# Hybrid linear-attention layer on one core: half of one projection's depth tiles placed between the two low-rank gate products of the first head pair

## What is computed

```python
cond = silu(c); mod = cond @ w_ada + b_ada            # 6 x 1024: shifts, scales, gates
h = modulate(rms_norm(x), shift1, scale1)
proj = h @ w_in     # GLA q,k (256 each), v (512), low rank (16), gate (512); HGRN2 q,f,i,gate (512 each)
gate_logits = g_lr @ gla_gate_w2 + gla_gate_b2        # (1024,16) @ (16,256)
log_a = log_sigmoid(gate_logits) / 16                 # decay of the GLA heads
# chunkwise causal linear attention with chunks of 64, for 4 GLA and 4 HGRN2 heads
x = x + gate1 * (concat(o_gla, o_hgrn) @ w_out)
x = x + gate2 * (square(relu(modulate(rms_norm(x)) @ w_mlp1)) @ w_mlp2)
return rms_norm(x, final_norm_g)
```

## Time and profile before

| | us |
|---|---|
| median of three executions | 1175.17 |
| the profiled execution | 1174.98 |
| its span | 1173.3 |
| PE busy | 1153.5 |
| DVE busy | 808.5 |
| ACT busy | 597.3 |
| POOL busy | 441.9 |

### The profile page before, as it was taken

How to read it: one execution, slowest core, us unless ns; L and a number is a source line. 1 busy time by engine, 2 the same in 40 slices (tenths; PEclk the granted TensorE clock), 3 DMA queues, 4 the chain that set the end, 5 groups by cost and what they waited for, 6 DMA issues and landing times.

```text
span 1173.3 us, 15641 instructions
## 1 busy us (share of the span) xinstructions
PE 1153.5 (98%) x5639; PEld 956.9 (82%) x5639; DVE 808.5 (69%) x957; ACT 597.3 (51%) x898; POOL 441.9 (38%) x273
## 2 busy tenths in 40 slices
PE   7999999999999999999999999999999999999996
PEld 6878788888888888888888888888878888888885
DVE  6998766554535458367987755676796785966876
ACT  7753554646464647245655555455663433424424
POOL 1021111111111215326444442435367574765751
PEclk9999999999999999999999999999999999999999
DMA  9675241021111114341355435534624737437203
GB/s 362 235 249 162 90 145 36 19 54 36 36 36 36 37 44 137 93 159 72 117 179 167 148 117 171 179 135 140 211 72 131 245 92 265 144 130 281 78 1 144
DMA packets 148765, 152.02 MB, mean 130 GB/s; under 512 B 6228, under 2 KB 117976, under 8 KB 146008
## 3 DMA queue, kind: packets, MB, share of 16 engines
q1 hardware_dynamic: 148696, 151.12, 39.4%
HBM read 117.02 MB, written 34.08 MB: 129 GB/s over the span
## 4 chain that ended last, share of the span: by engine, by line
PE 87%; DVE 5%; issue 3%; DMA 2%; ACT 1%; SPq 1%; DVEq 0%; ACTq 0%
PE unit_bank L1321 29%; PE unit_bank L1621 8%; PE unit_bank L1622 8%; PE unit_bank L1623 8%; PE small_bank L1621 8%; PE small_bank L1622 8%; PE small_bank L1623 8%; PE small_bank L1321 3%; PE small_bank L1456 2%; DVE ada_acc L1703 2%; DMA ada_slot<-in_w_ada_dram 1%; PE small_bank L1448 1%; PE small_bank L1360 1%; DVE state L1903 1%; DMA quarter<-in_w_mlp_dram 1%
## 5 line engine op out<-in xcount | busy, mean ns | idle before, releaser
L773 POOL TENSOR_TENSOR wr_lo<-quarter,wr_hi 128x512 fp32r<-128x512 f32 x122 | 196.0, 1620 | 174.3 <-ACT wr_hi L1122 174.2
L1321 PE MATMUL unit_bank<-a_hi,w_hi 128*128 128x512 f32 x560 | 223.2, 399 | 0.0
L1321 PE MATMUL unit_bank<-a_hi,w_lo 128*128 128x512 f32 x560 | 218.4, 390 | 0.0
L1321 PE MATMUL unit_bank<-a_lo,w_hi 128*128 128x512 f32 x560 | 218.1, 389 | 0.0
L717 POOL TENSOR_TENSOR w_lo<-raw,w_hi 128x1024 fp32r<-128x1024 f32 x27 | 67.5, 2501 | 347.8 <-ACT w_hi L827 347.8
L1621 PE MATMUL unit_bank<-op_hi,wr_hi 128*128 128x512 f32 x452 | 176.5, 391 | 0.6 <-DVE op_lo L2216 0.6
L1621 PE MATMUL small_bank<-op_hi,wr_hi 128*128 128x512 f32 x452 | 176.2, 390 | 0.0
L1623 PE MATMUL unit_bank<-op_hi,wr_lo 128*128 128x512 f32 x452 | 175.9, 389 | 0.0
L1623 PE MATMUL small_bank<-op_hi,wr_lo 128*128 128x512 f32 x452 | 175.9, 389 | 0.0
L1622 PE MATMUL unit_bank<-op_lo,wr_hi 128*128 128x512 f32 x452 | 175.9, 389 | 0.0
L1622 PE MATMUL small_bank<-op_lo,wr_hi 128*128 128x512 f32 x452 | 175.8, 389 | 0.0
(11 more groups left out here) (257 smaller groups left out, 1846.1 us busy)
## 6 DMA issues: line engine op xcount, KB each, us to landing
quarter<-in_w_mlp_dram SPq DMA_DIRECT2D x128, 256.0 KB, 4.4
hidden_scratch<-hid SPq DMA_DIRECT2D x98, 256.0 KB, 2.9
ada_slot<-in_w_ada_dram SPq DMA_DIRECT2D x48, 512.0 KB, 6.5
op_full<-hidden_scratch SPq DMA_DIRECT2D x21, 1024.0 KB, 4.8
raw<-in_w_in_dram SPq DMA_DIRECT2D x29, 512.0 KB, 3.9
raw<-in_w_out_dram SPq DMA_DIRECT2D x16, 512.0 KB, 4.0
x_stage<-in_x_dram SPq DMA_DIRECT2D x8, 512.0 KB, 5.1
x_scratch<-xT SPq DMA_DIRECT2D x2, 2048.0 KB, 8.2
```

The lines of the kernel that those rows point to most:

```text
L773: pool.tensor_tensor(wr_lo[slot][:, :, :], split_source(n), wr_hi[slot][:, :, :].bitcast(F32), ALU.subtract).then_inc(wr_lo_pool, 1)
L1321: return pe.matmul(out_ap, left, right, start=start, stop=stop)
```

## The change

The first four depth tiles (12 products) of unit 2, half 0, are issued between the two `z` pieces of step 0. Step 2 issues the remaining four. The number of products and their sums are the same.

```diff
-                        half_unit(u0 + j, 1 + j, half, a_hi, a_lo)
+                        half_unit(u0 + j, 1 + j, half, a_hi, a_lo, tiles=range(KH if name == "P0" and jj == 2 else 0, KT))
                     both = []
                     for p in steps[name][jj]:
                         b = p[3]
+                        if name == "P0" and p[0] == "z" and p[2] == 1:
+                            half_unit(u0 + 1, 2, 0, a_hi, a_lo, tiles=range(KH))
                         if b in used:
```

## The result

The change makes the kernel slower: 1177.86 us median of nine executions against 1175.05 for nine of the kernel before, ratio 1.0027, 95% interval 1.0019 to 1.0036, so +2.8 us. The executions lie from 1176.57 to 1180.81, those of before from 1174.67 to 1176.56. The range 1175.6 to 1180.8 holds the median; the point, 1179.1, is 1.2 too high. A second series, beside the experiments, gave 1178.82 against 1175.17 (six executions, ratio 1.0032, 1.0020 to 1.0045). One of the 22 executions of the kernel before in that second series took 1662.76 us, at a mean granted clock of 0.654, and is left out of the ratio.

The account below looks back on a forecast made before the run. TensorE, busy for 1153.5 of 1173.3 us, was taken as the bound. The profiled 1174.98 plus 2.1 (late unit 3) plus 1.9 (clock fall) gave 1179.0, and 0.19 for the median gave 1179.1 us; range 1175.6 to 1180.8.

Parts of the forecast that it names:

- Steps 1 and 2: Unit 2: TensorE through 1.54 us early; second `z` 1.27 late, its absolute value 1.19 late; POOL asks at 69.27.
- Step 3: Ahead of unit 3: POOL's subtraction waits for DVE's whole scan, ends at 73.14; unit 3 starts 2.1 us late.
- The row of the scan's tail: At 72.65 POOL met the scan's last 0.32 us and took 0.11 over 2.40; waiting would give 0.17.
- Step 4: Unit 3 to unit 5: the delay persists, at most some 0.3 us absorbed; +2.1 carried on.
- Step 5: At the hole ahead of unit 3: the granted clock falls to half, costing 1.9 us, kept between 1.3 and 3.4.
- if the clock stays at full through the hole: Sign against the forecast: no fall of TensorE's clock in the 3.4 us wait ahead of unit 3.
- first rival: Ahead of unit 3: POOL waits for the scan but the clock stays full; +2.1, 1177.3 us; chance 0.25.
- the cases within 0.2%: Whole kernel: part of wait without clock, plus POOL not held and the small gain; chance given as 0.34.
- The gain: Unit 3's low weights not late: 1.54 us early until DVE's `mod`, 0.3 of it kept; 1174.9 us; chance 0.06.

Follow-up runs that it names:

- e4: The change, with one DVE row addition of `w_ada` moved from ahead of log_a to behind it, just ahead of the scan; 1176.9 us, one execution.
- e3: The change, with ACT making unit 3's high weights before copying unit 1 out, in the first group alone; 1175.04 us, ratio 1.0001 to the kernel before.
- e5: The change itself run again, unmodified, to see its clock; 1178.82 us, ratio 1.0032 to the kernel before.
- e1: The change, with 14 extra unused products on TensorE in its wait ahead of unit 3; 1177.0 us, ratio 1.0017 to the kernel before.
- e6: The change with six products instead of twelve between the two gate products; 1175.26 us, one execution.

## Why the prediction was right, and where it was off

**Steps 1 and 2** held to the hundredths. By the ruler the absolute value of the second gate product starts at 3.86 (61.91 - 58.05) against 2.67 (60.55 - 57.88): +1.19. POOL asks at 11.38, forecast 69.27 - 57.88 = 11.39. DVE's log_a did not move (9.50 against 9.47): the additions of `w_ada` cover ln. In e4, where one of them is taken from there, DVE waits for ln and the cover is gone.

**Step 3**, POOL behind the scan, was right: 15.17 by the ruler, forecast 73.14 - 57.88 = 15.26. The row of the scan's tail, which I had called thin evidence, pointed the right way. The exclusion that the Trainium skill states ("SBUF — State Buffer", "Who interferes with whom") agrees with e3 and e4 as well: in every one of these the second to come waited for about all that was left of the first. Not quite all: POOL ended 2.13 to 2.25 us after the DVE instruction, and alone it takes 2.40, so, as an estimate, up to 0.27 us of its work was done by then.

**Step 4** was right: +2.1 forecast, 2.04 measured, and nothing of it was given back. DVE came out even (L1981 at 20.73 against 20.67 by the ruler).

**Step 5**, the clock, is the term that was off, in three ways. *Size:* I priced the fall at 1.9 and e5 shows 1.57. *Its picture:* I let the low time of 6.8 us begin with the hole, so that 3.4 were left for the work. In e5 the clock was full through the hole, and the low time was 3.4 us in all (74.0 to 77.4), every bit of it on the products behind. That my 1.9 is near the 1.57 is thus in part luck; the rows from which I took the rate were also of products of 128 columns, not of 512. *Whether it comes:* the sum takes the fall as certain, and one of two profiled executions with equal holes has it. I had named "if the clock stays at full through the hole" as a sign that the forecast is wrong, and the first profile shows just this, there and behind it. The rule that the Trainium skill states ("TensorE: Matmul & The Clock Gate", "HAM oscillation"), that a long enough idle gap brings the clock back to half, agrees with e5; the 3.35 us of the first profile did not do it, so at this length it can go either way.

The profiled execution is thus my first rival (wait without clock: 1177.3 forecast, 1177.26 measured), and the forecast itself, with 1.57 for 1.9, would be 1178.8, which is e5's execution (1178.86). The median of 1177.86 lies between the two, and that of the second series, 1178.82, close to the forecast. How many executions had the fall can't be said, since only two were profiled; the mean clocks of the others and e1 speak for the clock as the cause of the rest, but e1's four high executions show that other scatter takes part. That part of the account is argued, not shown.

Two slips of arithmetic moved little: 1178.98 and 0.19 make 1179.17 and not 1179.1, and the cases within 0.2% add up to 0.36 and not 0.34.

**The gain** as a rival: its cap was not exceeded. At unit 3 a gain can be had (0.27 in e6, 0.29 in e3), and at unit 5 nothing of it is left, where DVE's `mod` stands in front. I had thought that up to 0.3 would be kept; that the cap would hold 1.54 back was not tried as such.

## What to carry to other kernels

A hole on the full engine is cheap to fill only if nobody waits for the instruction behind it. Before putting work there, follow that instruction through the other engines to its last effect: here 1.2 us on ACT became 2.2 us on POOL, because a request that had come just ahead of a long DVE instruction came just behind its start. Once the hole is filled elsewhere it comes back at the next wait (unit 3, then unit 4, then `mod`), so the whole row of waits up to the next slack has to be opened, and then about 1 us is there (0.9 by the medians, 1.3 by the ruler), little against the 2 to 3.7 us that the unguarded change costs.

## What the runs showed that I had not expected

An identical empty stretch of TensorE (3.33 and 3.35 us) halved the clock in one execution and left it full in another. Work of no use in the hole, 14 products, cost no time, and by the medians of other series gave 1.2 us or more, which the intervals leave open. And DVE's place against TensorE at the same point of the program differs by 0.7 us between executions (scan at 10.02 and at 10.72 after ACT's copy), which is enough to change who waits for whom. The shift came in the three profiles in which the granted clock had fallen to half some 10 us ahead of the change.
